# A new table of steps: which expert steps stand at which places of the trunk, laid out by share of places passed

## The reference

```
for l in range(DEPTH):                    # 2 layers
    h = _rms(x, g_norm_mix[l]) * (1.0 + sc_m) + sh_m
    ...                                   # three branches, y_a, y_b, y_c
    x = x + gt_m * (merged @ w_out[l])
    h2 = _rms(x, g_norm_ffn[l]) * (1.0 + sc_f) + sh_f
    x = x + gt_f * _peer(h2, peer_w_q[l], peer_keys[l], peer_u[l], peer_v[l])

def _peer(...):                           # per token: 8 heads x 16 experts
    top_s, pos = lax.top_k(cand, PEER_TOPK)
    e_idx = jnp.take_along_axis(cand_idx, pos, axis=-1)
    gate = jax.nn.softmax(top_s, axis=-1)
    u_sel = u[e_idx]; v_sel = v[e_idx]
    act = gelu(einsum('thkd,td->thk', u_sel, xb))
    return einsum('thk,thkd->td', gate * act, v_sel)
```

## Time and profile before

| | us |
|---|---|
| median of three runs (4265.19 to 4279.12) | 4274.04 |
| the profiled execution, whole | 4273.03 |
| its span, first to last instruction | 4271.2 |
| PE busy | 3205.0 (75%) |
| DVE busy | 2479.4 (58%) |
| ACT busy | 1665.8 (39%) |
| bytes moved by DMA | 1315.65 MB, of these 1073.81 MB expert rows |

### The profile page before, as it was taken

The page is one execution under the profiler, slowest core; times in us unless marked ns, Lnnn a source line. Parts: engine busy times, 40 slices in busy tenths (PEclk is TensorE's granted clock), DMA queues, the critical chain, the costliest instruction groups (busy, mean ns, idle before and its releaser), DMA issues.

```text
span 4271.2 us, 64529 instructions
## 1 busy us (share of the span) xinstructions
PE 3205.0 (75%) x22584; PEld 1964.3 (46%) x22584; DVE 2479.4 (58%) x6208; ACT 1665.8 (39%) x4730; POOL 1135.3 (27%) x1028
## 2 busy tenths in 40 slices
PE   7788986478888986858988887467988985445444
PEld 4576773145545673424545575134554673111111
DVE  2322219977556617687645627978646717865544
ACT  2213113364465313343465423364466323333333
POOL 0000002344333001234433301434433101443332
PEclk8779997578888997758898998578898997555555
DMA  7302337999999438999999945999999634999997
GB/s 252 106 22 94 108 114 310 393 378 401 391 377 395 190 115 305 345 359 391 401 402 387 408 172 224 384 400 392 400 385 378 273 114 182 391 407 421 421 420 312
DMA packets 247588, 1315.65 MB, mean 308 GB/s; under 512 B 21216, under 2 KB 35168, under 8 KB 116192
## 3 DMA queue, kind: packets, MB, share of 16 engines
q0 software_dynamic: 147456, 1073.81, 62.1%
q1 hardware_dynamic: 99808, 237.72, 15.7%
HBM read 1309.34 MB, written 2.10 MB: 307 GB/s over the span
## 4 chain that ended last, share of the span: by engine, by line
PE 28%; DMA 24%; DVE 19%; PEld 8%; ACT 8%; issue 7%; DVEq 2%; ACTq 2%; PEldq 2%; POOL 0%; POOLq 0%; SPq 0%
DMA row<-uv,e_idx 19%; DVE row L1526 7%; PE bank L617 5%; PE bank L671 5%; PEld bank L657 3%; PE bank L1002 3%; DMA weights<-w_in 2%; DMA weights<-w_ada 2%; PEld bank L671 2%; DVE reg L1424 2%; PEld bank L934 2%; PE bank L657 1%; DVE reg L1419 1%; PE bank L850 1%; ACT e_diag L1098 1%
## 5 line engine op out<-in xcount | busy, mean ns | idle before, releaser
L1941 POOL DMA_INDIRECT row<-uv,e_idx x1024 | 1135.1, 1109 | 3099.1 <-PE bank L617 1739.8
L1526 DVE CUSTOM_DVE_ANT_0 row<-row,e_rep 128x1024 f32<-128x1024 f32 x1024 | 1243.1, 1225 | 677.5 <-DMA row<-uv,e_idx 622.5
L617 PE MATMUL bank<-row,e_diag 128*32 128x256 f32 x8192 | 871.8, 513 | 726.4 <-ACT e_diag L1098 697.9
L617 PEld LDWEIGHTS bank<-row,e_diag 128*32 128x32 f32 x8192 | 195.2, 125 | 1283.7 <-ACT e_diag L1098 1050.8
L1094 ACT ACTIVATE e_ge<-e_dot 128x1 f32<-128x1 f32 x1024 | 206.5, 202 | 1208.4 <-DVE e_dot L1526 1192.1
L671 PE MATMUL bank<-hT,weights 128*128 128x256 f32 (+2 forms) x2176 | 533.5, 401 | 41.6 <-ACT hT L1163 24.8
L671 PEld LDWEIGHTS bank<-hT,weights 128*128 128x128 f32 (+2 forms) x2176 | 411.2, 194 | 165.5 <-issue 53.9
L657 PE MATMUL bank<-hT,weights 128*128 128x256 f32 x1536 | 365.1, 387 | 14.3 <-issue 12.7
L1098 ACT ACTIVATE e_diag<-mask,e_wg 128x32 f32<-128x32 f32 x1024 | 329.1, 321 | 74.1 <-issue 4.0
L1096 ACT ACTIVATE e_wg<-e_gate,e_ge 128x1 f32<-128x1 f32 x1024 | 301.5, 294 | 74.0 <-issue 4.1
L657 PEld LDWEIGHTS bank<-hT,weights 128*128 128x128 f32 x1536 | 281.0, 190 | 98.1 <-issue 61.9
(11 more groups left out here) (270 smaller groups left out, 3871.3 us busy)
## 6 DMA issues: line engine op xcount, KB each, us to landing
weights<-w_ada SPq DMA_DIRECT2D x48, 1024.0 KB, 7.5
weights<-w_mac SPq DMA_DIRECT2D x64, 768.0 KB, 8.5
weights<-w_in SPq DMA_DIRECT2D x44, 1024.0 KB, 10.0
weights<-w_mb SPq DMA_DIRECT2D x32, 768.0 KB, 4.3
weights<-w_out SPq DMA_DIRECT2D x16, 1024.0 KB, 5.0
weights<-w_pq SPq DMA_DIRECT2D x16, 1024.0 KB, 5.0
row<-uv,e_idx POOLq DMA_INDIRECT x1024
weights<-w_in SPq DMA_DIRECT2D x8, 1056.0 KB, 18.2
```

The lines of the kernel that those rows point to most:

```text
L617: last = mm(acc_ps[g % 2][c * QT:(c + 1) * QT, 0:2 * P], e_diag[:, n % RING, :], row[n % RING][:, D + c * 2 * P:D + (c + 1) * 2 * P], star ...
L1526: V.tensor_tensor_reduce(row[r][:, 0:D], row[r][:, 0:D], e_rep[g % 2], 1.0, 0.0, ALU.mult, ALU.add, e_dot[:, r:r + 1]).then_inc(dots, 1)
L1941: pool.indirect_dma_start(row[r], None, uv, bass.IndirectOffsetOnAxis(ap=e_idx[:, j:j + 1], axis=0)).then_inc(rows_landed[r], 16)
```

## The change

The strings of `STEPS` are replaced, for all three engines and all three laps that carry steps. No instruction is added to or taken from the trunk or the steps; only their order on PE, ACT and DVE changes (the loads of ACT's function tables, which follow from the order of the functions, go from 229 to 197). POOL and SP keep their order.

```diff
@@ STEPS, first line of each string of the first of the three laps @@
     "PE": (
-        "100000000000011101030s00C001120203011110111110000010010080011100103001000100200100010001000211000011000001000100001000"
+        "10000000100020100301010100000000000200021210001000002002a0000000x00001000002100000110000020000000000001001000020001000"
...
     "DVE": (
-        "1000KJ0010010202311010001000130101001200100110010011110011010013101101001011101001001020012102100100110101000101011014"
+        "1021202050101010001111110111111101111201011111110111E00000000103002004000100000000200020002001000001000000000100000003"
```

More of the change, by code:

```diff
@@ new lines @@
+        "0000000000000000010000000000001000000000000000100001000100010101010000001000001100010001000101000100002010001010000001"
+        "0001000100010000030010001000002100000010001000020001200101100010111111100000000100000002210111301001000200331100200002"
+        "0000000000003000020000010000000000000100002300010010200310121101211011101011101011101011101012001012010100000400220100"
+        "00002101000000302010010200111011010101010010101010101300000010100101010101010103000001001010101010101100000100",
@@ new lines @@
+        "0111010111011010110112110120100101013000000100010000011000000002010000000000000104001000111011110121101010100103000000"
+        "10100101010100101013000000001010101001010100000001",
+        "1000111000001030011010000000020000022200002101000002000090000000x00001000002100000110000010000000000002001000020001000"
+        "0000000000000000000000001000001000000000000000100003000100000001010000000001001000010010000101000100101001001000001000"
+        "0010000010000010000011003000000100010030010010000003000101100001012111010000000000000003110111101112000100312201100102"
@@ new lines @@
+        "303220300000001203025010000002001000013010001000800000000062200010g001333100302012111202003140101111051140401011122112"
+        "0110200000142101000616101010411010210000232101000000000001000343202020202020202020303020302004000200000300000000010000"
+        "131001202020303020201004010001030100011100000006000000000100010010",
+        "301010000011015000000001000000402010000301002000000023D001332100203000201000004000101102030220201020222421021010001004"
+        "1100000505110210611010211001121101000000001000000000011121022040202030402020202020202030040205000005000001000510102111"
@@ new lines @@
+        "0021000011011010002010110031130011101061001080000000d10010070202000000500000000000001000101111002000110013011100110011"
+        "011001100110011001100110011001110102010201030111011101111d020202010401010310130012160011110",
+        "8530000040240601000020300000500010110700000035300200000000000100j00000000103002004000100000000200020003003100001100000"
+        "0011011211021020101000203001001010300111021002011140010010a0000100c000100703010000008000000000000060020020020020020020"
+        "020110020020030030020120020100000001010011010118020203030202010310131012150001110",
@@ L296 @@
+        "1400303050000010100014010100140102000201011111110111E00000000103002002000110000000200020002002000000000000000101000002"
+        "0021000101110100100101100120031021202040010170001001b00020080301000000600000000000001001101011002000110012003000120011"
+        "001101100110011001100110011001110101011010101130101111011e020202020302020310040012160011110",
     ),
```

42 lines of the change are left out of this document (10 added, 32 removed).

## The result

The kernel with the new table takes 4141.24 us (median of four runs, 4132.51 to 4152.7), the kernel before 4269.61 us beside it (four runs, 4261.32 to 4279.12). The ratio is 0.9697, 95% interval [0.9672, 0.9722]: 128 us, or 3.0%, faster. The forecast was 4247, with a range of 4175 to 4325.

A forecast was written before the change was run, and what follows sets the result against it. DVE and DMA were taken to bound the openings, PE and DMA in balance behind them. Terms -86 -33 -34 -41 -1 +57 +50 +62 summed to -26, from 4273 to 4247 us; range 4175 to 4325.

The forecast's parts named there:

- The late terms: Attentions +57, second merges +50 and ends +62 us, for the steps moved into these stretches.
- I take DVE's price: Openings of laps 1 and 3: 36 fewer steps at 1.19 us of DVE, 43 us each, -86 for both.
- bounds of 25 and 90: Gain per opening, laps 1 and 3: 25 us if DVE waits more for projections' copies, 90 if gathers bound it.
- isn't a new cost: Openings: the block of 30 steps before the recurrence adds nothing, as the same steps stood in a block before.
- taking steps away cannot give more than the PE price: From the recurrence on, PE and DMA are in balance and a step costs about PE's 0.93 us.
- Recurrences and middles: Recurrences: 40 fewer steps at 0.84 us, -34; middles: 37 fewer at 1.1 us, -41.
- The ends: Last stretch of each lap: 67 more steps at 0.93 us, +62.
- PE's 14 idle us: End of the lap: PE is busy 72 of 86 us, and its idle time can take some steps.
- slower in series: Rival: attention and end steps delay a chain through DVE, ACT and PE, 1.7 us each; +44, 4317 us; chance 0.3.
- The larger gain: Rival: late steps hide in PE's idle time and openings give 55 us each; -123, 4150 us; chance 0.2.
- What was to show the forecast right: Lengths expected per stretch in the changed kernel's profile, and POOL's wait on L1500 down by over 400 us.
- the openings' lower bounds: In the no-change rival (chance 0.13): the openings give only -66 us instead of -119.

The follow-up runs named there:

- x1: Mixed table: the new table's openings, with steps as dense as in the old table behind them; 4196.51 us, ratio 0.981 to the kernel before.
- x2: Mixed table: the old table's openings (97, 73, 97 steps), with the new table's places behind them, thinned; 4241.65 us, ratio 0.9925 to the kernel before.
- x4: New table, but the 61 steps in the openings of laps 1 and 3 laid out in the old table's manner; 4194.41 us, ratio 0.9831 to the kernel before.
- x5: New table with 22 steps moved on from middles and lap 2's recurrence to later stretches; 4187.1 us, ratio 0.9774 to the kernel before.

## Why the prediction was wrong

**The direction and the map were right.** Early stretches gave, late ones paid, in the order of the forecast. The late terms came out at +187 against +169, DVE's work in the opening of lap 1 fell by 46 against 43. x1 and x2 show that such a sum over stretches holds. That the late terms are so near is in part luck: the attentions and second merges came out lower, the ends 31 us higher, and most of the prices were read as PE's time, which the runs do not bear out.

**The step that failed first** is "I take DVE's price" in the openings of laps 1 and 3, -86. As to the number of steps it was about right (1.28 us measured in before's layout, 1.19 forecast). But I read DVE's 44 idle us as a constant of the opening. They were mostly the difference to a second limit that I had computed in the bound (90 us an opening) and set aside: the rows' 279 us. With 61 steps it is 196, and the idle time goes, if the order lets it. The openings gave 73 and 82 us, inside the bounds of 25 and 90. By size nearly all of the 69 us missed here lies in the layout, which the forecast set at nothing ("isn't a new cost"): it is worth 33 us an opening at 61 steps, 65 of the 155 us (x4 against after), while the number of steps alone gave 46 an opening for the forecast's 43.

**The second** is "taking steps away cannot give more than the PE price". Recurrences and middles gave 1.35 and 1.9 us a step, 124 us for the forecast's 75. Here the number was an average (from no steps to 68), used for the last 17. Before's recurrence ran at a DMA share of 1.00, 68 steps in 180 us or 2.65 each, the pace of steps alone. That the last step costs there what its row costs, until the stretch meets its next limit, is an argument from these numbers; halved rows gave only 10, 15 and 3 us in the three recurrences. With whole rows, six buffers and nothing else changed, lap 1 took 150 to 157 us with 42 to 51 steps and 179 to 184 with 68: nearly flat, then some 1.6 us a step. Lap 3 is less clear, 145 to 164 us with 40 to 49 steps.

In the middles the new table also saves loads of ACT's function tables, 21 in lap 1 for 35, at 1.28 us each. They are not the reason for 1.9 us a step: from after to x2 the three middles have 19 steps fewer with the same number of loads, within one, and take 36 us less, again 1.9 a step.

And the price was not PE's alone: with 231 us of PE's time gone the kernel was 11 us faster. The Trainium skill (page "Perfetto Trace Analysis", its opening note) calls matmul busy time a bad metric for how close a kernel is to roofline, because matmuls are pipelined. No run here tests that reason, but this case too had read too much from PE's busy time: two of four matmuls less, and PE was as busy as before (3206.5 against 3205.0 us).

**The ends** were mis-sized the other way, +93 for +62, 1.39 us a step. PE's 14 idle us took none of it. In lap 1 PE's busy time grew by 25 us (72 to 97 of 119, with the clock at 0.86 instead of 0.94), and its idle time by 8 more, with the DMA share at 0.74: nothing there is full. A finished diagonal waits 10.7 us there for its sum in the mean, against 3.4 in the recurrence, and DVE waited 41 us in all for rows. So the steps pay in waits in order and in clock. The rival "slower in series" was right in kind for this stretch alone, and its 1.7 a step was not reached.

**The rivals.** The larger gain, 4150 at its full size, came nearest, but by another mechanism: no late steps were hidden in idle time; the early stretches gave more. The Trainium skill's rule that performance may be improved by interleaving regimes (page "Perfetto Trace Analysis", section "Optimization Strategy") gave the right side: 128 us less. What was to show the forecast right was met in attention (66 us), second merge (64) and POOL's wait, and missed in opening (218 for 240 to 260), recurrence (152 for 162 to 168), first merge (121 for 124 to 126) and end (119 for 105 to 109). Two sums of the rivals are slightly off: half of the larger gain is 4198 by its terms and not 4190, and the openings' lower bounds add up to -64 and not -66. Nothing hangs on either.

**What stays open:** what a step behind the opening pays with. Half the rows, half the dot and narrower matmuls each gave little there, and no two of them were tried together. Open with it are why x5's late steps cost 3.7 us, how the 1.39 us of the ends split between the clock, DVE, ACT and the row buffers, and how much of after's recurrence is PE's.

## What to carry to other kernels

Before pricing work that moves out of a stretch, write down for that stretch each engine's busy time and DMA's (share times length): the greatest is its floor, and a moved item can give back its part of the floor until the next limit, and more or less than that by the order. In the openings this was nearer than the part of the busiest engine or the average since the stretch was bare. Two limits within a few per cent hide each other in experiments that relieve only one. In an order written out by hand, the distance between an item's places on two engines is as much a parameter as the number of items: one place on PE, in the recurrences, cost 57 us here.

## What the runs showed of the hardware

- Four matmuls that write four different groups of 32 PSUM partitions cost PE no more time than two: 4096 instructions fewer left PE busy 3206.5 us instead of 3205.0.
- With narrower matmuls the granted clock was lower: 0.760 to 0.764 over the span in all ten executions on before's table against 0.785 to 0.795 of before beside them, 0.804 to 0.772 on after's in the profiles, and 0.88 to 0.73 in one recurrence, where the stretch became 17 us longer though PE had less to do.
- The clock of a recurrence differs between executions of the same instructions: lap 0's, without steps, took 123 us at 0.77 and 134 at 0.70.
- A gathered row's round trip is no constant. With six buffers the steps alone take 685 us from the end of the trunk to the last sum, with five 708, with six of half the bytes 538.
- The one core in use drew 402 to 420 GB/s over stretches of 120 to 180 us, at a DMA share of 1.00 to 1.01.
